# TensorE goes past six stage barriers, and SyncE loads the position bias of a two-layer hybrid backbone

## The chip, the cores and the metric

The kernel runs on one core of one Trainium2 chip. The metric is the device time of one execution in microseconds, as the median of three runs.

## The reference, cut to what matters

Two layers run over 256 context and 256 latent tokens of width 1024, all in float32. Each layer does:

```python
h = rms_norm(x, g1) * (1 + sc1) + sh1             # the same for the context
p = h @ w_in                                       # feeds three mixers and three merge gates
y_a = mlstm_branch(...)                            # chunkwise mLSTM, both directions
y_b = mla_branch(...)                              # latent attention with a rotary part
y_c = natten_branch(...)                           # neighbourhood attention with a position bias
y = (sig(g_a) * y_a + sig(g_b) * y_b + sig(g_c) * y_c) @ w_out
x = x + g1 * y
x = x + g2 * (relu(norm2(x) @ w_ff1) ** 2 @ w_ff2)
```

In the neighbourhood attention a latent query row adds a bias to its scores against the latent keys, and a mask shuts out columns beyond its window:

```python
bias = rpb[:, dr_idx[None, :, None], dc_idx[:, None, :]]
s_win = q @ k_band * scale + bias
s_win = where(col_ok, s_win, NEG_INF)
s_ctx = q @ k_ctx * scale                          # no bias, no mask
p = softmax(concat([s_win, s_ctx]))
```

The last layer computes latent tokens only; its context serves as keys and values.

## The kernel before, in words

Every product is made from float32r halves: a weight block `raw` is split into `wH` (ScalarE, line 710) and `wL = raw - wH` (GpSimd, lines 579 and 581; for some blocks VectorE does the first part, line 1082), and TensorE forms `wH*xH + wH*xL + wL*xH`. Weight blocks pass through a ring of 17 quarters of 256 columns. A 1 MB block (eight quarters) of the neighbourhood attention, `na` 0 to 5, so finds room for two at a time. SyncE loads the blocks in one written order (`load`, line 484); a block's load waits until the block that held its place is split, and its split waits until TensorE has used that block.

A layer is a row of stages, each written out by hand for each engine: `ml` (mLSTM), `na`, `mla`, and then without barriers between them the merge (`to`, `wo`) and the MLP (`ff`). At the end of `ml`, `na` and `mla`, in each of two layers, ScalarE, VectorE, GpSimd and TensorE all call `end()`: a drain that adds 1 to the semaphore `phase_end` and a wait until it holds 4 for each barrier so far (function `barrier`, lines 558 to 561). A seventh one stands at the end of the kernel. SyncE waits on `phase_end` in one place only (in `load_gate`, before it loads gate tiles of the merge into memory that the `mla` stage used).

GpSimd splits blocks ahead before it comes to `end()`: at the end of `ml` it splits `na` 0 and then `na` 1, at the end of `na` the block `dq` 1, while VectorE at the end of `mla` makes the first parts of four `to` blocks. TensorE waits before each product for its weights (`w_split`, `w_share`) and before it fills a bank for the bank's last reader (`bank_free`).

The `na` stage: units 0 to 5 are the products with `na` 0 to 5 (lines 1665 on), queries first, then keys, then values. ScalarE squares each bank (line 956), VectorE sums and scales it (lines 1397, 1413, 1422), and TensorE turns it round (line 1849). Then come the attention steps (scores at line 1888). At the start of the stage ScalarE issues 12 DMAs for the bias table `a_tb` (line 869; 128 KB each, rows of 64 floats), since that memory holds mLSTM values until the barrier. VectorE waits for all 12 and adds the mask in one instruction over 3072 columns (line 1314) before it sums any bank. The table is read at line 1461, in the attention steps of latent tiles.

Of the kernel before, what the change touches and what calls it, by code (L numbers as in the profile page):

```python
# [25 lines left out]
ALU = mybir.AluOpType  # L26
# [258 lines left out]
def build(nc, a, out):  # L285
    ctx = ExitStack()
    with ctx:
# [187 lines left out]
        def _(sp):  # L475
# [19 lines left out]
            def load_gate(l, T):  # L495
# [14 lines left out]
                    sp.wait_ge(*S(f"gate_out{k}").at(16 * KC * (l + 1)))  # L510
                sp.dma_start(dst, g_spill[K, :, lat]).then_inc(S(f"gate_in{c % 2}" if branch == 2 else f"gate_b{c}").handle, 16)

            def load_all(name, l, js):
                for j in js:
                    load(name, l, j)
# [12 lines left out]
            for l in range(DEPTH):  # L528
                if l:
                    load_all("ml", l, range(7))  # L530
                cn = gate_range(l, "cn").start
                for T in range(cn):
                    load("gate", l, T)
                    if l == 0 and T in (3, 4, 7, 8):
                        load_mod(MOD_PROJ + (3, 4, 7, 8).index(T))
                load_all("na", l, range(6))
                load_all("ns", l, range(KC))
                for key in KEYS[N["dq", l, 0]:N["ms", l, 0]]:
                    load(*key)
                load_all("ms", l, range(KC))  # L540
                load_all("to", l, range(4))
                for branch in (2, 1):
                    for c in range(KC):
                        load_gate(l, TURN.index((branch, c)))
                load_all("wo", l, range(4))
                for j in range(32):
                    load("ff", l, j)
                    if l == 0:
                        for m in ff_mods(j - 2):
                            load_mod(m)  # L550
# [93 lines left out]
        def _(act):  # L644
# [147 lines left out]
            for l in range(DEPTH):  # L792
# [63 lines left out]
                for br in ("na", "mla"):  # L856
# [2 lines left out]
                    nb = list(norm_banks(br, l))  # L859
                    if br == "na":  # L860
                        act.preload_act_table_set("sqrt_and_others")
                        for j in range(6):
                            for up in range(2):

                                src = bass.AP(a["na_rpb"].tensor,
                                              a["na_rpb"].offset + l * HEADS * RPB_R * RPB_C
                                              + (WIN_R - GRID_H + 1 + j - up) * RPB_C + WIN_C - GRID_W,
                                              [[1, GRID_W], [RPB_R * RPB_C, HEADS], [1, GRID_W]])
                                act.dma_start(a_tb[64 * up:64 * up + 64, :, j, :], src)\
                                    .then_inc(S(f"na{l}_rpb").handle, 16)  # L870
                    if br == "mla":
                        for j in range(3):
                            ahead(N[("dq", l, j) if j < 2 else ("dk", l, 0)])
# [177 lines left out]
        def _(dve):  # L1051
# [121 lines left out]
            for l in range(DEPTH):  # L1173
# [129 lines left out]
                for br in ("na", "mla"):  # L1303
# [3 lines left out]
                    if br == "na":  # L1307
                        dve.tensor_scalar(gcols[:, 0:1], par[:, l, R_NGQ:R_NGQ + 1], NA_SCALE, None, ALU.mult)
                        dve.tensor_copy(gcols[:, 1:2], par[:, l, R_NGK:R_NGK + 1]).then_inc(S(tag + "g").up(1), 1)
                        kk = S(tag + "g").n  # L1310
                        dve.wait_ge(*S(tag + "rpb").at(12 * 16))
                        mask = const[:, C_MASK:C_MASK + GRID_W].rearrange("p (a w) -> p a w", a=1)
                        tb = a_tb.rearrange("p h j w -> p (h j) w")
                        link(dve.tensor_tensor(tb, tb, mask.broadcast_to([P, 48, GRID_W]), ALU.add))
                    else:
                        dve.memset(gcols[:, 0:1], MLA_SCALE)
                        link(dve.memset(gcols[:, 1:2], 1.0))
                        dve.tensor_scalar(gcols[0:64, 0:1], par[0:64, l, R_GQ:R_GQ + 1], MLA_SCALE, None, ALU.mult)
                        dve.tensor_copy(gcols[0:64, 1:2], par[0:64, l, R_GK:R_GK + 1]).then_inc(S(tag + "g").up(1), 1)
                        kk = S(tag + "g").n  # L1320

                        free(dve.tensor_copy(l_c[:, 4, :], full(u0 + 2, 0)[:, :]), u0 + 2, 0)
                        freed(u0 + 2, 0)
                        free(dve.tensor_tensor(l_c[:, 4, :], l_c[:, 4, :], full(u0 + 2, 1)[:, :], ALU.add), u0 + 2, 1)
                        freed(u0 + 2, 1)
                        dve.wait_ge(*S(tag + "cstd").at(2))
                        for c in range(5):
                            lo = t0 if c < 3 else 0
                            dve.scalar_tensor_tensor(l_c[:, c, lo:], l_c[:, c, lo:],
                                                                      par[:, l, R_GCQ + c:R_GCQ + c + 1],  # L1330
                                                                      st[:, int(c >= 3), lo:], ALU.mult, ALU.mult).then_inc(S(tag + "cn").up(1), 1)
                        dve.wait_ge(*S(tag + "cn").at(5))
                        for c in range(5):
                            lo = t0 if c < 3 else 0
                            dve.wait_ge(*S(tag + "cH").at(c + 1))
                            dve.tensor_tensor(oL[:, C_AT[c], lo:], l_c[:, c, lo:],
                                                               oH[:, C_AT[c], lo:].bitcast(F32), ALU.subtract).then_inc(S(tag + "cL").up(1), 1)
                        dve.wait_ge(*S(tag + "cL").at(5))
                        for t in range(NTILE):
                            dve.wait_ge(*S(tag + "krs").at(t + 1))  # L1340
                            dve.reduce_sum(stat[:, 32 + t:33 + t], l_t[:, 0:ROPE], axis=AX).then_inc(S(tag + "krsum").up(1), 1)
                            kr = l_kr[:, t:t + 1, :]
                            link(dve.tensor_tensor(kr, small[:, t:t + 1, 32:64], ropeg[:, l, 1:2, :], ALU.mult))
                            if t >= 2:
                                rope(kr, kr, l_r, t - 2, 1)
# [91 lines left out]
                    for m in range(len(nb) + 1):  # L1437
# [4 lines left out]
                        if m >= 2:  # L1442
                            keys_out(m - 2)
                    keys_out(len(nb) - 1)

                    items = [(qi, t, h) for qi, t in enumerate(att_tiles(l)) for h in range(HEADS)]
                    for step in range(len(items) + 3):
# [122 lines left out]

        @block.tensor
        def _(pe):
            phase = [0]

            def end():
                phase[0] += 1
                barrier(pe, phase[0])

            def begin(u, b):

# [123 lines left out]
            for l in range(DEPTH):  # L1704
# [91 lines left out]
                    ins.then_inc(S(tag + "nd").up(1), 1)  # L1796
                square_sums(ML_H - 1)
                gates(l, "last")
                end()
                for br in ("na", "mla"):  # L1800
                    tag = f"{br}{l}_"
                    u0 = U0[br, l]
# [116 lines left out]
                                                   flip if br == "na" else ident)  # L1919
                            ins.then_inc(S(tag + "ot").up(1), 1)  # L1920
                    assert next(extra, None) is None and pace * len(items) >= 12 * KC
                    end()

                for j in range(4):
                    features(N["to", l, j], U0["to", l] + j, 4, both(4, t0), oH, oL)
# [19 lines left out]
                            square_sums2(1, 0, 0, 2 * (j - 5))  # L1945
                if l == 0:
                    square_sums2(1, 0, 0, 6)
            end()
            for k in range(4):
                for c in range(4):  # L1950
                    cc = (k % 2) * 4 + c
# [59 lines left out]
```

## Time and profile before

| | |
|---|---|
| median of three runs | 1999.97 us (1999.17 to 2003.4) |
| the profiled execution's own time | 2001.05 us |
| its span | 1998.9 us |
| TensorE matmul busy | 1706.2 us (85%) |
| VectorE / ScalarE / GpSimd busy | 1034.3 / 835.2 / 671.7 us |
| mean granted TensorE clock | 0.937 |

The profile's page gives busy time by engine, the chain that ended last, and the groups of instructions with the idle time before them. A wait at line 560 is a wait at a stage barrier; the engine named is the one that came last.

### The profile page before, as it was taken

How to read it: one execution, taken by the hardware profiler on the slowest of the kernel's cores; microseconds unless marked ns; L12 is line 12 of the kernel's file. 1: busy time of each engine (PE TensorE's matmuls, PEld its weight loads, DVE VectorE, ACT ScalarE, POOL GpSimd, SP SyncE). 2: the span in 40 equal slices, each digit the busy share in tenths (PEclk: the TensorE clock that was granted, in tenths of full speed). 3: DMA queues.
4: the chain of work that ended last, by engine and by line, in shares of the span. 5: the costliest groups of instructions: out<-in, count | busy, mean ns of one | idle time of the engine just before them, and what ended most of it. 6: DMA issues, size and time to landing. Idle time of an engine off the chain costs nothing.

```text
span 1998.9 us, 24815 instructions
## 1 busy us (share of the span) xinstructions
PE 1706.2 (85%) x9538; PEld 1437.7 (72%) x9538; DVE 1034.3 (52%) x1851; ACT 835.2 (42%) x1474; POOL 671.7 (34%) x420
## 2 busy tenths in 40 slices
PE   2578798899887898889999998978788878879998
PEld 1466576886666666658888886867786666678998
DVE  6797843225324444445868874145134245445565
ACT  3214465334354542243223233268434366435443
POOL 1323322440133300144555543523452333023442
PEclk8789899999998999999999999989899888989999
DMA  6364211420012303214344653121321123154553
GB/s 256 136 232 179 96 37 42 117 85 22 22 61 80 131 23 125 91 43 160 121 182 171 250 211 126 59 95 59 116 85 64 55 88 116 43 182 143 176 188 127
DMA packets 66216, 229.58 MB, mean 115 GB/s; under 512 B 18465, under 2 KB 22707, under 8 KB 52531
## 3 DMA queue, kind: packets, MB, share of 16 engines
q1 hardware_dynamic: 46992, 208.42, 29.4%
q10 hardware_dynamic: 19107, 19.58, 3.0%
q8 instruction: 76, 1.25, 0.2%
q14 instruction: 41, 0.34, 0.1%
HBM read 216.45 MB, written 11.53 MB: 114 GB/s over the span
## 4 chain that ended last, share of the span: by engine, by line
PE 67%; DVE 15%; ACT 8%; issue 4%; POOL 2%; DMA 1%; ACTq 1%; POOLq 1%; DVEq 0%; SPq 0%
PE bank L1609 35%; PE bank L1665 8%; PE bank L1621 6%; PE bank L1909 4%; DVE acc L1100 3%; PE bank L1794 3%; DVE mjunk L1097 3%; PE bank L1888 3%; PE bank L1895 2%; PE bank L1647 2%; ACT wH L710 2%; POOL wL L579 1%; DVE arena L1128 1%; POOL hL L597 1%; PE bank L1849 1%
## 5 line engine op out<-in xcount | busy, mean ns | idle before, releaser
L710 ACT ACTIVATE wH<-raw 128x768 fp32r<-128x768 f32 (+7 forms) x396 | 296.7, 806 | 598.0 <-PE bank L1609 399.8
L579 POOL TENSOR_TENSOR wL<-raw,wH 128x1280 fp32r<-128x1280 f32 (+4 forms) x146 | 300.3, 2057 | 698.2 <-ACT wH L710 698.2
L581 POOL TENSOR_TENSOR wL<-raw,wH 128x768 fp32r<-128x768 f32 (+3 forms) x198 | 319.8, 1615 | 397.6 <-ACT wH L710 397.6
L1609 PE MATMUL bank<-hH,wH 128*128 128x512 f32 (+1 forms) x848 | 302.1, 356 | 88.0 <-DVE hL L1137 34.7
L1609 PE MATMUL bank<-hL,wH 128*128 128x512 f32 (+1 forms) x848 | 296.9, 350 | 0.0
L1609 PE MATMUL bank<-hH,wL 128*128 128x512 f32 (+1 forms) x848 | 296.1, 349 | 0.0
L1609 PEld LDWEIGHTS bank<-hH,wH 128*128 128x128 f32 x848 | 167.7, 198 | 116.9 <-issue 57.0
L1609 PE MATMUL bank<-oH,wH 128*128 128x512 f32 (+1 forms) x576 | 196.6, 341 | 9.9 <-DVEq L560 9.9
L1609 PE MATMUL bank<-oL,wH 128*128 128x512 f32 (+1 forms) x576 | 195.3, 339 | 0.0
L1609 PE MATMUL bank<-oH,wL 128*128 128x512 f32 (+1 forms) x576 | 195.1, 339 | 0.0
L1609 PEld LDWEIGHTS bank<-hH,wL 128*128 128x128 f32 x848 | 167.7, 198 | 19.1
L1609 PEld LDWEIGHTS bank<-hL,wH 128*128 128x128 f32 x848 | 168.0, 198 | 18.5 <-issue 0.5
L1100 DVE SCALAR_TENSOR_TENSOR acc<-acc,cb 128x1024 f32<-128x1024 f32 x96 | 176.7, 1852 | 2.7
L1621 PE MATMUL bank<-hH,wH 128*128 128x512 f32 (+1 forms) x384 | 148.3, 386 | 13.8 <-ACT gst L737 7.9
L1665 PE MATMUL bank<-wH,hH 128*128 128x256 f32 x480 | 140.4, 293 | 17.6 <-POOLq L560 14.8
L1665 PE MATMUL bank<-wL,hH 128*128 128x256 f32 x480 | 138.9, 289 | 0.0
L1665 PE MATMUL bank<-wH,hL 128*128 128x256 f32 x480 | 138.8, 289 | 0.0
L1621 PE MATMUL bank<-hL,wH 128*128 128x512 f32 (+1 forms) x384 | 136.8, 356 | 0.0
L1621 PE MATMUL bank<-hH,wL 128*128 128x512 f32 (+1 forms) x384 | 136.7, 356 | 0.0
L1525 DVE SCALAR_TENSOR_TENSOR arena<-bank,modT,arena 128x256 f32<-128x256 f32 x120 | 54.3, 480 | 140.5 <-PE bank L1609 139.4
L1609 PEld LDWEIGHTS bank<-oH,wH 128*128 128x128 f32 x576 | 110.8, 192 | 22.3 <-DVEq L560 10.3
L1609 PEld LDWEIGHTS bank<-oL,wH 128*128 128x128 f32 x576 | 110.9, 193 | 11.8 <-issue 0.5
(212 smaller groups left out, 3242.1 us busy)
## 6 DMA issues: line engine op xcount, KB each, us to landing
raw<-in_p_ff SPq DMA_DIRECT2D x64, 1024.0 KB, 4.8
acc<-in_p_mod SPq DMA_DIRECT2D x48, 1024.0 KB, 5.4
raw<-in_p_ml SPq DMA_DIRECT2D x12, 1024.0 KB, 6.9
raw<-in_p_na SPq DMA_DIRECT2D x12, 1024.0 KB, 4.8
raw<-in_p_mgc SPq DMA_DIRECT2D x16, 512.0 KB, 3.9
raw<-in_p_mga SPq DMA_DIRECT2D x16, 512.0 KB, 3.5
raw<-in_p_mgb SPq DMA_DIRECT2D x16, 512.0 KB, 3.4
raw<-in_p_out SPq DMA_DIRECT2D x8, 1024.0 KB, 7.8
```

The costliest lines, as they stand in the source:

```text
L579: pool.tensor_tensor(l_[:, 0:cut], r_[:, 0:cut], h_[:, 0:cut].bitcast(F32), ALU.subtract)
L581: pool.tensor_tensor(l_[:, cut:k * w], r_[:, cut:k * w], h_[:, cut:k * w].bitcast(F32), ALU.subtract)\
L710: act.activation(flat(wH, n)[:, part], flat(raw, n)[:, part], ACT.Copy)\
L1097: link(dve.scalar_tensor_tensor(mjunk[:, :], row, 1.0, cb[:, LAT, :], ALU.mult, ALU.mult, accum_out=modT[:, l, chunk, LAT:LAT + 1]))
L1100: ins = dve.scalar_tensor_tensor(row, row, 1.0, cb[:, last, :], ALU.mult, ALU.mult, accum_out=modT[:, l, chunk, last:last + 1])
L1525: ins = dve.scalar_tensor_tensor(x[:, c + b, lo:lo + 256], src[:, lo:lo + 256], modT[:, l, gate + c + b, s:s + 1], x[:, c + b, lo:lo + 256 ...
L1609: ins = pe.matmul(dst, w_[:, kk, c:c + P], r_[:, kk, lo:TOK], start=kk == k0 and m == 0, stop=kk == k0 + kn - 1 and m == 2)
L1621: ins = pe.matmul(bank[gate_bank(l, T)][:, t0:TOK], w_[:, kk, :], r_[:, kk, t0:TOK], start=kk == 0 and m == 0, stop=kk == KC - 1 and m == 2)
L1665: ins = pe.matmul(bk[:, o:o + width], s_[:, at[kk], t * P:t * P + P], w_[:, kk, c:c + width], start=kk == 0 and m == 0, stop=kk == k - 1 a ...
L1794: ins = pe.matmul(bank[bk][:, lo:hi], lhs, m_E[d][:, e_at, 0:hi - lo], start=q == 0, stop=q == len(group) - 1)
L1888: pe.matmul(bank[4 + step % 2][:, 0:nk], q_, k_, start=True, stop=True).then_inc(S(tag + "s").up(1), 1)
L1909: ins = pe.matmul(bank[k % 2][:, 0:P], s_pt[:, k % 2, c * P:c * P + P], v_[:, c, (h // 2) * P:(h // 2) * P + P], start=c == 0, stop=c == n ...
```

## The change

TensorE no longer waits on `phase_end` at the six stage ends. It still adds its 1, so that the other three engines wait for it as before, and then waits for semaphores of the stage it leaves: at the end of `ml` for ScalarE's and VectorE's last work on its banks and for the gates of the `ml` loop; at the end of `na` and `mla` for the last bank of the branch product and for `oL`, which reads the last turned bank. Only at the end of the kernel does it wait on `phase_end` as before. The four other engines' barriers stay.

The 12 bias DMAs move from ScalarE to SyncE, between the loads of `na` 2 and `na` 3, behind a wait until the barrier after `ml` has passed. The mask is added behind the last normalised keys, just ahead of the attention steps.

```diff
+            def load_bias(l):
+
+                for j in range(6):
+                    for up in range(2):
+                        src = bass.AP(a["na_rpb"].tensor,
+                                      a["na_rpb"].offset + l * HEADS * RPB_R * RPB_C
+                                      + (WIN_R - GRID_H + 1 + j - up) * RPB_C + WIN_C - GRID_W,
+                                      [[1, GRID_W], [RPB_R * RPB_C, HEADS], [1, GRID_W]])
+                        sp.dma_start(a_tb[64 * up:64 * up + 64, :, j, :], src).then_inc(S(f"na{l}_rpb").handle, 16)
+
...
-                load_all("na", l, range(6))
+                load_all("na", l, range(3))
+                sp.wait_ge(S("phase_end").handle, 4 * (3 * l + 1))
+                load_bias(l)
+                load_all("na", l, range(3, 6))
...
-                        for j in range(6):
-                            for up in range(2):
...
-                                act.dma_start(a_tb[64 * up:64 * up + 64, :, j, :], src)\
-                                    .then_inc(S(f"na{l}_rpb").handle, 16)
...
-                        dve.wait_ge(*S(tag + "rpb").at(12 * 16))
-                        mask = const[:, C_MASK:C_MASK + GRID_W].rearrange("p (a w) -> p a w", a=1)
-                        tb = a_tb.rearrange("p h j w -> p (h j) w")
-                        link(dve.tensor_tensor(tb, tb, mask.broadcast_to([P, 48, GRID_W]), ALU.add))
...
                     keys_out(len(nb) - 1)
+                    if br == "na":
+                        dve.wait_ge(*S(tag + "rpb").at(12 * 16))
+                        mask = const[:, C_MASK:C_MASK + GRID_W].rearrange("p (a w) -> p a w", a=1)
+                        tb = a_tb.rearrange("p h j w -> p (h j) w")
+                        link(dve.tensor_tensor(tb, tb, mask.broadcast_to([P, 48, GRID_W]), ALU.add))
...
-            phase = [0]
-
-            def end():
-                phase[0] += 1
-                barrier(pe, phase[0])
+            def leave():
+
+                pe.drain().then_inc(S("phase_end").handle, 1)
...
-                end()
+                leave()
+                pe.wait_ge(*S(tag + "std").at(ML_H))
+                pe.wait_ge(*S(tag + "acc").at(2 * ML_H))
+                pe.wait_ge(*S("gate_free").at(GATES * l + gate_range(l, "loop").stop))
...
-                    end()
+                    leave()
+                    pe.wait_ge(*S("branch_free").at(tiles_so_far(br, l) + KC))
+                    pe.wait_ge(*S(tag + "oL").at(len(att_tiles(l))))
...
-            end()
+            leave()
+            pe.wait_ge(S("phase_end").handle, 4 * (3 * DEPTH + 1))
```

## Rows read from the trace of the kernel before

**Rows 1.** The chain that ended last: shares of the span by engine.
```profile
PE 67%; DVE 15%; ACT 8%; issue 4%; POOL 2%; DMA 1%; ACTq 1%; POOLq 1%; DVEq 0%; SPq 0%
```

**Rows 2.** TensorE's waits, whole run: total us, times, longest us.
```profile
PE bank L1665 <- POOLq L560: 14.8, 2, 8.2
PE bank L1609 <- DVEq L560: 9.9, 2, 4.9
PE bank L1609 <- POOLq L560: 7.0, 2, 3.5
PE bank L1849 <- DVE arena L1422: 5.5, 2, 5.0
```

**Rows 3.** Timeline at the first barrier: start us, us, instruction, [idle before].
```profile
350.78 1.82 POOL L581 TENSOR_TENSOR wL<-raw,wH 128x768 fp32r<-128x768 f32 x1
...
356.15 1.80 POOL L581 TENSOR_TENSOR wL<-raw,wH 128x768 fp32r<-128x768 f32 x1
358.06 9.51 ACTq L869 DMA_DIRECT2D arena<-in_na_rpb  x12
358.07 0.58 PE L1665 MATMUL bank<-wH,hH 128*128 128x256 f32 x1 [6.63 <-POOLq L560]
370.48 3.36 DVE L1314 TENSOR_TENSOR arena<-arena,const 128x3072 f32<-128x3072 f32 x1 [12.21 <-DMA arena<-in_na_rpb]
```

**Rows 4.** The chain in order of time, layer 0: start us, us, work.
```profile
358.07 25.47 PE bank L1665 x192
384.41 11.51 PE bank L1665 x96
...
534.14 28.91 PE bank L1609 x120
...
886.01 321.95 PE bank L1609 x1419
```

**Rows 5.** The chain in order of time, layer 1.
```profile
1293.07 1.28 ACT wH L710
...
1299.22 6.01 PE bank L1609 x48
...
1469.62 11.52 PE bank L1665 x96
...
1569.53 22.10 PE bank L1609 x120
```

**Rows 6.** Timeline at the fourth barrier, layer 1, after `ml`.
```profile
1429.16 1.80 POOL L581 TENSOR_TENSOR wL<-raw,wH 128x768 fp32r<-128x768 f32 x1
...
1435.66 10.02 ACTq L869 DMA_DIRECT2D arena<-in_na_rpb  x12
...
1448.98 4.59 DVE L1314 TENSOR_TENSOR arena<-arena,const 128x3072 f32<-128x3072 f32 x1 [13.12 <-DMA arena<-in_na_rpb]
1450.31 4.93 POOL L581 TENSOR_TENSOR wL<-raw,wH 128x768 fp32r<-128x768 f32 x1
```

**Rows 7.** Time to landing: `na` weight blocks in 350 to 400 us, bias DMAs.
```profile
DMA to landing us min/median/max: 4.7/5.1/5.9
...
DMA to landing us min/median/max: 3.4/3.9/5.9
```

**Rows 8.** Timeline of VectorE at the first attention scores of layer 0.
```profile
437.77 0.43 DVE L1465 TENSOR_REDUCE stat<-bank 128x1 f32<-128x256 f32 x1 [14.96 <-PE bank L1888]
```

**Rows 9.** Timeline of VectorE ahead of the second barrier, after `na`.
```profile
531.38 0.69 DVE L1482 TENSOR_TENSOR oL<-bank,oH 128x512 fp32r<-128x512 f32 x1 [1.38 <-ACT oH L1004]
```

**Rows 10.** Timeline at the third and sixth barriers, after `mla`.
```profile
781.20 3.55 DVE L1082 TENSOR_TENSOR wL<-raw,wH 128x768 fp32r<-128x768 f32 x4
...
802.39 1.62 DVE L1502 TENSOR_TENSOR acc<-acc,arena 128x512 f32<-128x512 f32 x1
...
810.05 0.69 DVE L1502 TENSOR_TENSOR acc<-acc,arena 128x512 f32<-128x512 f32 x1
...
1758.46 2.00 ACT L710 ACTIVATE wH<-raw 128x1280 fp32r<-128x1280 f32 x2 [18.22 <-DMA raw<-in_p_out]
```

More of the change, by code:

```diff
@@ L861, in _ @@
                         act.preload_act_table_set("sqrt_and_others")
-                        for j in range(6):
-                            for up in range(2):
[L865 to L868, printed above, removed]
-                                act.dma_start(a_tb[64 * up:64 * up + 64, :, j, :], src)\
-                                    .then_inc(S(f"na{l}_rpb").handle, 16)
                     if br == "mla":
```

## The prediction

> **What bounds the kernel now.** I read the page's chain first: TensorE holds 67% of it [rows 1], and a matmul is running for 85% of the span. So time can only be saved where TensorE stands still or runs at its lower clock. Second, the list of its waits [rows 2]. The six stage barriers cost it 14.8 + 9.9 + 7.0 = 31.7 us, two waits for each kind of stage end. In four of them GpSimd came last, in two VectorE. A fourth entry, 5.0 us before a turn (line 1849), is one wait of layer 1. These 37 us are the ground that the change can work on. Third, the timelines at each barrier, to see what TensorE could have started on, since a wait that goes is replaced by the next one.
>
> **Barrier 1, after `ml` of layer 0.** TensorE waits 6.63 us until GpSimd has split `na` 0 and then `na` 1 [rows 3]. Unit 0 needs only `na` 0, done at 350.78 + 1.82 = 352.60. The three new waits are for work of ScalarE and VectorE that was over before. So unit 0 starts at about 352.7 and not at 358.07: 5.4 us. `na` 1 is done at 357.95 and unit 1 wants it only 11.5 us after 352.7. The first two units take 25.47 us for 192 matmuls, later ones 11.51 for 96 [rows 4], so 25.47 - 23.02 = 2.4 us went to the lower clock (1.2 GHz of 2.4) after the 6.6 us of idling. With only 1.2 us of idling left I expect the clock to stay up. Sum 7.8 us; bounds 5.4 (clock still falls) and 7.9.
>
> Who could spoil this? Behind the start stand ScalarE, whose squares no longer queue behind 9.51 us of DMA issue, and VectorE, which no longer waits for the bias: both only get earlier. `na` 2 is loaded before the new wait on SyncE. `na` 3 is not: it now stands behind the barrier (358.0) and 12 DMA issues. SyncE has no such DMA in this trace; the nearest row is ScalarE's own issue, 9.51 and 10.02 us for 12, and I take that. `na` 3 is then issued at 367.6 and lands 5.1 us later [rows 7], at 373. TensorE uses `na` 1 up to 352.7 + 23.0 = 375.7, and only then may `na` 3 be split, so its load is covered by 3 us; and from raw data to TensorE a split takes 1299.22 - 1293.07 = 6.15 us [rows 5], half of what unit 2 covers. Cost in layer 0: nothing; without the cover it would be each microsecond of lateness beyond 381.
>
> **Barrier 4 and the start of `na` in layer 1.** `na` 0 is split at 1429.16 + 1.80 = 1430.96 [rows 6]; TensorE starts at 1435.67 after 8.2 us [rows 2] of waiting. Here units 0 and 1 have half the rows (48 matmuls each), so the stage is tight. Before, the bias came in at 1448.98, the mask took VectorE 4.59 us, GpSimd's split beside it took 4.93 in place of 1.80, and TensorE waited 5.0 us for VectorE [rows 2, 6]. All that goes: ScalarE and VectorE are free from 1435.6. Unit 3 started at about 1469.4 [rows 5]. Now units 0 to 2, 192 matmuls, need 23.0 us at full clock, plus 0.7 for the turns, plus at most the 2.4 that layer 0 lost: from 1431.0 that is 1454.7 to 1457.1. The other condition is `na` 3: issued at 1435.6 + 9.6 = 1445.2, landed at 1450.3, split 6.1 later, at 1456.5 to 1457. The DMA decides here. Gain at unit 3: 1469.4 - 1457 = 12.4; because nothing covers a late load here I take 11.5. Bounds: 12.5, and 8.6 if the load lands 3 us later. The nearest thing to that is a queue that gives `na` 3 nothing until the bias has landed: last issue at 1444.6, landed 3.9 later [rows 7] at 1448.5, then 5.1 to 5.9 for the block: 1454.4 at worst, 4 us later than my value.
>
> The Trainium skill, page "DMA: Bandwidth & Descriptors", section "Queues, rings and completion order", speaks against this step: an engine's hardware queue is one ring on each transfer engine, taken in ring order, while different queues are served in turn. By it the weight block that shared the engines with the bias before (ScalarE's queue and SyncE's) stands behind it now. By that rule layer 1 gains 3 us less and layer 0 nothing less; by a plain 5.1 us after issue it is the sum above.
>
> **The mask in its new place.** VectorE idles 14.96 us before the first scores [rows 8]; 3.4 to 4.6 us of mask fit in that, also with GpSimd slowed by 3 us beside it, since its next small blocks are used in the attention steps only. Cost 0; without cover 4.6 a layer. In layer 1 the gap is of the same kind.
>
> **Barriers 2 and 5, after `na`.** `oL` ends at 531.38 + 0.69 = 532.07 [rows 9], TensorE started at 534.14, and its weights `dq` 0 were split long before. It now starts at 532.15: 2.0 us. At barrier 5 the same rows stand 1035.3 us later: 2.1. The clock: 120 matmuls took 28.91 us, at the rate of the MLP (321.95 / 1419 = 0.227) they take 27.2, so 1.7 was lost [rows 4]; in layer 1 72 of 256 columns at 0.12 and 48 at 0.227 make 19.5, against 22.10 [rows 5], 2.6 lost. Idling falls from 3.4 to 1.4 us, in a stretch where TensorE was thinly used just before. I take half back, 0.9 and 1.3, with bounds of 0 and all. Sum 2.9 + 3.4 = 6.3; bounds 4.1 and 8.4.
>
> **Barriers 3 and 6, after `mla`.** TensorE waits 4.9 us each for VectorE, whose four `to` splits take 3.55 us from 781.20 [rows 10]. It needs only the first (0.9): start at 782.1, not 784.86, 2.75 us. In layer 0 VectorE is next late: tied up until 802.39 + 1.62 = 804.0 by a split whose block lands no earlier, it then needs three more pairs of 1.4 us and ends at 808.3 and not 810.74. 2.4 us. In layer 1 nothing: the merge waits for the block of `w_out`, which lands at 1758.46 after 18.2 us of ScalarE's waiting [rows 10] and is issued behind SyncE's own `phase_end`, which VectorE still sets. Bounds 1 and 2.75 for the pair.
>
> **The sum.** 7.8 + 11.5 + 6.3 + 2.4 = 28.0 us. The profiled execution's own time was 2001.05 (span 1998.9 and 2.15 around it), so it would be 1973.0; it stood 1.1 above the median, so I name 1972. Everything between the barriers is paced by TensorE, so an earlier start is carried on; the MLP of 322 us without a break [rows 4] shows it best. All lower bounds together, 5.4 + 8.6 + 4.1 + 1.0 = 19.1, give 1981; all upper ones, 7.9 + 12.5 + 8.4 + 2.75 = 31.5, 1968.
>
> **Rivals.**
> - *The clock is given nothing and `na` 3 is late.* The starts move but the clock falls as before, and the load waits for the bias to land. For it: `na` 3 is the one transfer moved behind 1.5 MB of short rows. Against: idling at barrier 1 falls to a fifth. 5.4 + 8.6 + 4.1 + 2.4 = 20.5: 1979.5.
> - *Given back.* TensorE comes early to banks and blocks that others release no earlier, as in layer 1's merge, and only the mask's 5.0 us is kept: 1995. For it: barrier 6. Against: in `na` the next releases (squares, splits) hang on TensorE's own banks.
> - *SyncE's bias issue blocks the weights (the other side).* Place: `na` 3 behind 12 DMAs. If SyncE needs much longer than ScalarE's 9.5 us for them, TensorE waits for unit 3. Unit 3 started at about 396.5 in layer 0 (384.41 + 11.51 and the turns [rows 4]) and 1469.4 in layer 1; the load must be issued by 385 and 1458, so from about 25 us of issue the two `na` stages lose, and, with the 8.7 us of the other barriers against it, from about 29 the kernel does. At 38 us (four times ScalarE's): unit 3 at 407 and 1485, 10.5 + 15.5 - 8.7 = 17 slower: 2017. For it: SyncE's rate for such short rows isn't in the trace. Against: ScalarE's queue took 9.5 and 10.0 for the same transfers.
> - *TensorE does not get past.* A wait that I take as long over is not: a new wait stands behind GpSimd as `phase_end` did. Again only the mask: 1995.
>
> **Chances.** Forecast 70% (its own spread 1968 to 1977); clock and load 18%; given back 6%; blocked weights 3%; not past 3%. The 80% range is 1967.5 to 1983. About 0.2% (4 us) is what a measurement can tell from no change: faster 94%, same 3%, slower 3%.
>
> **What would show each step.** Right: line 560 gone from TensorE's waits; unit 0 starting within 0.2 us of the end of the first `na` split; 192 matmuls in about 23.0 us in layer 0; no wait of line 1849 in layer 1's first turn; unit 3 of layer 1 starting on GpSimd's split, with ScalarE's line 710 waiting for the DMA of `na` before it; barrier 6's gain eaten by `w_out`. Wrong: a wait of line 1888 for the mask; `na` 3 issued more than 12 us after the barrier; the first units after barriers 2 and 5 as slow as before; an early start followed by an equal wait at the next turn.

## The result and the profile after

The changed kernel takes 1979.5 us (median of 4 runs, 1977.6 to 1981.4) against 2001.7 us of the kernel before (4 runs, 1999.2 to 2003.6): ratio 0.989, 95% interval 0.987 to 0.991. The forecast of 1972 is 7.5 us too low. The 80% range (1967.5 to 1983) holds the time, the forecast's own spread (1968 to 1977) doesn't. The profiled execution's own time is 1979.92 us, its span 1977.8, so the span fell by 21.1 us where the steps promised 28.0.

TensorE's waits in the changed kernel, to be read against [rows 2] (engine, line and what it waited for: total us, times, longest):

```profile
PE bank L1612 <- DVE hL L1520: 18.1, 2, 10.5
...
PE bank L1668 <- POOL wL L594: 10.5, 5, 3.7
...
PE bank L1612 <- DVE wL L1086: 5.0, 2, 2.5
...
PE bank L1612 <- DVE oL L1487: 2.9, 2, 1.5
```

The three entries for a barrier, six waits in all, and the one for layer 1's turn are gone. In their place stand the data waits of the stages' first units: GpSimd's split (line 594), VectorE's split (1086), the last `oL` (1487). The largest of those shown is `hL` (1520), which ends the merge; it stood there before too (17.8 us in two waits, the longest 11.5). Ends of the `mla` stages, both layers, timeline of TensorE:

```profile
775.34 0.47 PE L1612 MATMUL bank<-oH,wH 128*128 128x512 f32 x1 [2.48 <-DVE wL L1086]
...
806.61 0.77 PE L1612 MATMUL bank<-hH,wH 128*128 128x512 f32 x1 [7.63 <-DVE hL L1520]
...
1721.31 0.55 PE L1612 MATMUL bank<-oH,wH 128*128 128x256 f32 x1 [2.48 <-DVE wL L1086]
...
1748.58 0.55 PE L1612 MATMUL bank<-hH,wH 128*128 128x256 f32 x1 [10.51 <-DVE hL L1520]
```

TensorE leaves after the first of VectorE's four splits, as forecast, 2.48 us after its last work and not 4.9. Then it waits 7.63 and 10.51 us at the end of the merge (6.31 and 11.54 before).

The first barrier, timelines of GpSimd, TensorE, SyncE (its DMA issues), ScalarE and VectorE, answering to [rows 3] and [rows 8]:

```profile
353.47 1.82 POOL L594 TENSOR_TENSOR wL<-raw,wH 128x768 fp32r<-128x768 f32 x1
...
355.54 0.36 PE L1668 MATMUL bank<-wH,hH 128*128 128x256 f32 x1 [1.41 <-POOL wL L594]
...
360.86 8.16 SPq L521 DMA_DIRECT2D arena<-in_na_rpb  x12
369.06 4.80 SPq L484 DMA_DIRECT2D raw<-in_p_na  x2
...
362.15 0.60 ACT L960 ACTIVATE arena<-bank 128x512 f32<-128x512 f32 x1
...
418.00 3.35 DVE L1449 TENSOR_TENSOR arena<-arena,const 128x3072 f32<-128x3072 f32 x1
418.04 4.18 POOL L592 TENSOR_TENSOR wL<-raw,wH 128x384 fp32r<-128x384 f32 x1
...
433.61 0.42 DVE L1470 TENSOR_REDUCE stat<-bank 128x1 f32<-128x256 f32 x1 [12.26 <-PE bank L1894]
```

TensorE starts 0.25 us after the first split. The mask fits ahead of the first scores with 12.26 us to spare, though the GpSimd split beside it takes 4.18 us (its neighbours of the same size take 1.01).

The chain in order of time, whose pieces answer to [rows 4] and [rows 5] (start us, us, work, number of instructions):

```profile
355.54 23.27 PE bank L1668 x192
378.81 0.87 PE bank L1855 x8
379.69 11.51 PE bank L1668 x96
...
528.30 27.46 PE bank L1612 x120
...
1424.86 8.70 PE bank L1668 x48
...
1439.82 11.78 PE bank L1668 x96
1451.60 0.44 PE bank L1855 x4
1452.04 11.52 PE bank L1668 x96
...
1549.86 21.27 PE bank L1612 x120
```

192 matmuls in 23.27 us: the clock stayed up (25.47 before). After the `na` stages the 120 matmuls take 27.46 and 21.27 us, not 28.91 and 22.10. Layer 1's `na` start, answering to [rows 6]: SyncE's issues, ScalarE's split of `na` 3 and GpSimd's end of it:

```profile
1429.36 8.74 SPq L521 DMA_DIRECT2D arena<-in_na_rpb  x12
1438.14 11.84 SPq L484 DMA_DIRECT2D raw<-in_p_na  x3
1443.51 2.01 ACT L723 ACTIVATE wH<-raw 128x1280 fp32r<-128x1280 f32 x2 [2.99 <-DMA raw<-in_p_na]
...
1447.77 1.86 POOL L594 TENSOR_TENSOR wL<-raw,wH 128x768 fp32r<-128x768 f32 x1
```

The weight blocks that SyncE issued between 1436 and 1440 us, from the view of their tile:

```profile
DMA to landing us min/median/max: 5.3/5.8/6.3
```

`na` 3 is issued behind the twelve bias DMAs and split 5.4 us later; it is ready at 1449.6, and TensorE wants it at 1452.04. It never waits for it.

**Where the missing microseconds went.** By the marks in both traces the steps brought 27.8 us (table further down). The rest was lost between them. The largest piece stands in a stage that the change doesn't touch, the `ml` stage of layer 1 from its first matmul to the last head's. Its row in the view by stretches, first the kernel before, then the changed one (stretch: length, busy time of each engine, granted clock, DMA share, GB/s):

```profile
1246.10:1415.80 169.70, 141.80 (x896) 128.62 (x896) 64.67 (x143) 98.51 (x165) 68.09 (x59) 0.91 0.22 75
```

```profile
1236.50:1410.30 173.80, 146.66 (x896) 132.89 (x896) 64.51 (x143) 98.52 (x165) 68.00 (x59) 0.89 0.21 73
```

The same 896 matmuls are busy 4.9 us longer, the other four engines the same to 0.2 us. The trace's record of the granted clock, which has two levels, 1.2 and 2.4 GHz, puts 29.7 us of this stage at 1.2 GHz before and 37.5 after. That was the open question for the experiments: is this the change's doing, or that of the moment at which the stage begins?

### The profile page after: what moved, and what is told of

It is laid out like the page before. It is cut to its first block, busy times and chain, and to the rows that moved or that the text cites. A ratio compares the mean times of both kernels' runs of the same rounds, so it can differ in the third digit from the quotient of the medians.

```text
span 1977.8 us, 24823 instructions
## 1 busy us (share of the span) xinstructions
PE 1707.5 (86%) x9538; PEld 1437.1 (73%) x9538; DVE 1032.7 (52%) x1851; ACT 835.3 (42%) x1474; POOL 674.6 (34%) x420
## 4 chain that ended last, share of the span: by engine, by line
PE 67%; DVE 15%; ACT 9%; issue 4%; POOL 2%; DMA 2%; ACTq 1%; DVEq 0%; SPq 0%
PE bank L1612 34%; PE bank L1668 8%; PE bank L1624 6%; PE bank L1915 4%; DVE acc L1104 3%; PE bank L1797 3%; DVE mjunk L1101 3%; PE bank L1894 3%; PE bank L1901 2%; PE bank L1650 2%; ACT wH L723 2%; DMA raw<-in_p_out 1%; DVE arena L1132 1%; POOL hL L610 1%; PE bank L1855 1%
## 5 line engine op out<-in xcount | busy, mean ns | idle before, releaser
L592 POOL TENSOR_TENSOR wL<-raw,wH 128x1280 fp32r<-128x1280 f32 (+4 forms) x146 | 306.8, 2101 | 674.3 <-ACT wH L723 674.3
```

Source lines behind the costliest of these rows:

```text
L592: pool.tensor_tensor(l_[:, 0:cut], r_[:, 0:cut], h_[:, 0:cut].bitcast(F32), ALU.subtract)
```

## The experiments

Every kernel ran beside the kernel before on its chip, and its ratio is to those runs (their medians were 2001.1 to 2004.5 us, so ratios compare better than medians). "ml 1" is the length of the stage just shown and, in brackets, how much of it was at 1.2 GHz. The last column says how long before the stage's first matmul the granted clock fell to 1.2 GHz, by the same record.

| kernel | median us | ratio (95%) | ml 1 us | clock fell ahead of it, us |
|---|---|---|---|---|
| before, first and second trace | 2002.1 (second) | 1.000 (0.999 to 1.001) | 169.6 (29.7), 169.6 (29.7) | 5.9, 5.8 |
| changed, first trace | 1979.5 | 0.989 (0.987 to 0.991) | 173.8 (37.5) | 3.4 |
| after_again | 1980.4 | 0.990 (0.988 to 0.992) | 173.9 (37.6) | 3.3 |
| bar_only | 1991.8 | 0.996 (0.994 to 0.997) | 169.9 (30.0) | 5.3 |
| bias_only | 1996.9 | 0.997 (0.996 to 0.998) | 169.6 (29.7) | 5.9 |
| bias_last | 1981.0 | 0.990 (0.988 to 0.991) | 173.9 (37.6) | 3.4 |
| pad2 | 1976.5 | 0.986 (0.985 to 0.988) | 170.0 (30.0) | 5.2 |
| pad5 | 1985.0 | 0.991 (0.989 to 0.992) | 173.3 (36.8) | 4.2 |
| wo_early | 1969.7 | 0.983 (0.982 to 0.985) | 169.6 (29.6) | 6.0 |
| wo_again (the same kernel) | 1969.9 | 0.984 (0.983 to 0.986) | 171.1 (31.5) | 6.1 |
| wo_mid | 1975.5 | 0.987 (0.986 to 0.988) | 171.2 (31.5) | 6.1 |
| before_pad1 | 2005.7 | 1.001 (1.000 to 1.003) | 172.2 (35.7) | 3.3 |
| wo_before | 2001.3 | 0.999 (0.998 to 1.000) | 169.6 (29.7) | 5.9 |

**The changed kernel again (after_again).** No edit.

> The changed kernel once more, whole. The six steps at the barriers measured 27.8 us in the first pair of traces (7.4, 3.4, 2.6, 11.2, 2.8, 0.4), but the time fell by 22.2: outside the steps the changed kernel's trace is 2.7 us later at the end of the first mLSTM stage, 0.9 in the first neighbourhood attention, 1.1 and 2.3 at the start and in the second mLSTM stage. Theory A (the lower TensorE clock falls in other places from run to run, nothing of the change): the six steps repeat within 1 us each, the four losses outside do not repeat in the same places, ratio 0.986 to 0.990. Theory B (the change itself costs these 7 us, by where its shifts put TensorE's idle spells): the same four losses of about the same size stand in this trace too, ratio 0.989.

The same ratio, and the same 173.9 us with 37.6 at the lower clock. Up to TensorE's arrival at the first barrier the first trace took 354.1 us, this one 350.9, the two traces of the kernel before 351.4 and 352.7. So the start-up was scatter and the `ml` 1 loss is not. The spans are equal all the same (1977.8 and 1977.6 us): of the 3.2 us that the second trace gains there it loses 1.7 in layer 1's `mla` stage, which has 39.4 us at 1.2 GHz and not 34.3, and 0.8 behind the last merge. What a stage takes in a single trace is thus good to 2 or 3 us, unless it repeats as `ml` 1's does.

**The barriers alone (bar_only).** The position bias back on ScalarE's queue and the mask ahead of the keys, in the changed kernel:

```
+                        for j in range(6):
+                            for up in range(2):
+                                ...
+                                act.dma_start(a_tb[64 * up:64 * up + 64, :, j, :], src)
```

> Barriers alone: TensorE passes the six barriers, ScalarE issues the bias DMAs and the mask is added first, as before. Theory A (the steps as predicted): layer 0 keeps all but about 1 us of its 7.4 at the first barrier, because the mask ends at about 374 on the clock of the trace before and TensorE's first turn wants VectorE by 376. Layer 1 keeps nothing at the fourth barrier: TensorE starts 4.7 us earlier and then waits about 10 for the mask, unit 3 starts where it did. Sum 6.4 + 3.4 + 2.6 + 0 + 2.8 = 15 less whatever is lost outside: ratio 0.9925 to 0.995. Rival (parts add up, the mask's own wait of 5.0 us is all that the bias is worth): 22 - 5 = 17 faster, ratio 0.9915, and TensorE's wait before the turn stays 5 us.

It gained 8.6 us (0.4%, interval 0.3 to 0.6), less than the 0.5% to 0.75% that I had expected. Layer 1 in its timelines of ScalarE's queue, VectorE, GpSimd and TensorE shows why:

```profile
1426.81 10.97 ACTq L879 DMA_DIRECT2D arena<-in_na_rpb  x12
1437.88 0.38 ACT L966 ACTIVATE arena<-bank 128x256 f32<-128x256 f32 x1 [9.80 <-issue]
...
1440.40 5.19 DVE L1324 TENSOR_TENSOR arena<-arena,const 128x3072 f32<-128x3072 f32 x1 [13.39 <-DMA arena<-in_na_rpb]
...
1442.34 4.92 POOL L591 TENSOR_TENSOR wL<-raw,wH 128x768 fp32r<-128x768 f32 x1
...
1447.11 0.69 PE L1860 MATMUL bank<-const,arena 128*128 128x128 f32 x2 [11.58 <-DVE arena L1432]
```

TensorE crosses the barrier early and then waits 11.58 us for VectorE at the first turn, because the bias is issued, landed and masked as late as ever. In layer 0 the same costs 3.11 + 0.77 us. Counted from TensorE's arrival at the barrier, unit 3 starts 1.7 us earlier than in the kernel before in layer 0, where I had expected 6.4, and 2.1 us later in layer 1, where I had expected no change; that is the miss. An earlier start without the bias's move is a wait moved by one unit: my "given back" rival, true for this half of the change.

**The bias alone (bias_only).** The kernel before with the bias loaded by SyncE (behind `phase_end`, ahead of `na` 3) and the mask behind the last keys; the barriers stay.

> Bias and mask alone: all engines keep the six barriers, SyncE loads the bias and the mask is added last. Theory A: layer 0 gains nothing (TensorE never waited for the mask there); layer 1 loses the wait of 5.0 us before the turn and the 1.2 us of lower clock behind it, unit 3 starts about 6.6 us earlier: ratio 0.9967. With the barriers alone at 15 that leaves some 5 us that need both parts. Rival (only the wait itself): 5 us, 0.9975. Rival (weights behind the bias in SyncE's queue cost something): a wait of TensorE or ScalarE for the load of the fourth block appears in layer 1, 0.999 or more.

5.8 us by the ratio, as expected. Layer 1's turn no longer waits, and units 0 to 2 take 26.9 us, not 33.7. The parts together, 8.6 + 5.8 = 14.4, fall 6 us or more short of the whole change's 20 to 22, though the whole has the `ml` 1 loss of 4.2 us and neither part has it. Each of the three is known to some 3 us. So part of the gain comes only where both are there, and the 11.58 us above are the largest place of it.

**The bias behind the weights (bias_last).** The rule that would make `na` 3 late behind the bias can be tried by putting all six `na` blocks first:

```
-                load_all("na", l, range(3))
+                load_all("na", l, range(6))
                 sp.wait_ge(S("phase_end").handle, 4 * (3 * l + 1))
                 load_bias(l)
-                load_all("na", l, range(3, 6))
```

> The changed kernel with the bias DMAs behind the load of the last of the six blocks (na 5) in place of ahead of the fourth: no weight block stands behind the barrier or the bias. Theory A: the fourth block (na 3) lands early, ScalarE's wait of 3.0 us for it in layer 1 goes, but TensorE did not wait for it (its split was done at 1449.6, unit 3 started at 1451.8), so the time stays within 0.5 us of the changed kernel. Rival (the load decides unit 3, as the prediction held): 2 to 3 us faster. Rival (the bias now lands late, since na 5 is issued about 32 us after the barrier and the mask must be on before the first scores 60 us after it): it still lands 20 us before, no cost.

No gain: 0.990 both. The place of `na` 3 behind the bias costs nothing.

**Work added ahead of the stage (pad2, pad5).** Two or five matmuls on TensorE near the end of layer 0's MLP; their result is overwritten by the next sum:

```
                         if l == 0 and i == 3 and j > 4:
+                            if j == 5:
+                                pe.wait_ge(*S("nrm10_sq").at(1))
+                                for _ in range(2):
+                                    pe.matmul(bank[4][:, 0:TOK], ones, n_sq[:, 0, 0:TOK], start=True, stop=True)
                             square_sums2(1, 0, 0, 2 * (j - 5))
```

> The changed kernel with two matmuls of 512 columns added on TensorE (their result is overwritten) near the end of the layer-0 feed-forward stage, where TensorE is never waiting: 2 x 0.43 = 0.86 us, all of it before the layer-1 mLSTM stage. In the three traces with the whole change that stage (start and heads) has 37.6 us at the lower granted clock, in the kernel before 29.7, and it is 4.2 us longer there (95.08 + 78.78 against 93.96 + 75.67). Theory B: the work of the stage is the same, and how much of it gets the lower clock hangs on when the stage begins; a later start by 0.86 us then changes the 37.6 us at the lower clock, by anything up to the 8 us between the traces (some 4 us of time), and the kernel ends between 3.5 us faster and 2 us slower than the changed kernel. Rival: the change itself leaves TensorE idle longer in that stage, whatever its start; then 37.6 us stay, and the kernel is 0.9 us slower than the changed one (ratio to before 0.9898 + 0.0004).

> The same with five matmuls, 5 x 0.43 = 2.15 us before the layer-1 mLSTM stage. Theory B: the start lies then where it lay in the kernel with the barriers alone, which had 30.0 us at the lower clock in this stage; I expect 28 to 32 us here, the stage 3.5 to 4.5 us shorter than in the changed kernel, and the total 1.3 to 2.3 us below the changed kernel's (ratio to before 0.988 to 0.9892). Rival (the stage's own waits set the lower clock, not its start): 37.6 us stay, and the total is 2.2 us above the changed kernel's (ratio 0.991).

One such matmul is two matmul records in the trace and costs 0.84 us, twice what I had reckoned: the MLP stage grew from 368.13 to 369.81 and 372.39 us. With 1.7 us of work more, the kernel is faster than the changed one (0.9864, interval 0.9848 to 0.9879, against 0.9898, 0.9880 to 0.9917), and the stage is back to 170.0 us. Between pad2's span and that of the changed kernel's first trace, 1971.9 and 1977.8 us, the stage accounts for 3.8 us less the pad's 1.7. The start-up, which scatters, is 5.1 us shorter (349.0 against 354.1 us up to the first barrier), and 1.4 us are lost again in other stages.

```profile
1232.90:1402.90 170.00, 142.32 (x895) 129.00 (x895) 64.56 (x143) 98.41 (x165) 68.19 (x59) 0.91 0.22 75
```

With 4.3 us more it has 36.8 us at the lower clock again, and the kernel is 1.4 us slower than the changed one by the ratios, 5.1 by the spans. The stage's work is the same in all; only what stands ahead of it changed. My guess for pad5, 28 to 32 us at the lower clock and a gain, was made with half the length of the five and missed. Together the two show that the loss comes and goes with what is put ahead of the stage. That the change itself makes TensorE idle more in this stage is refuted by pad2.

**The same on the kernel before (before_pad1).** One such matmul, 0.84 us.

> The kernel before, untouched but for one matmul of ones on the squares (f32, two passes, 0.84 us by the length that two and five of them gave the layer-0 feed-forward stage: 1.68 and 4.26 us) near the end of that stage. Theory B (what part of the layer-1 mLSTM stage gets the lower granted clock hangs on when the stage begins, in the kernel before as in the changed one): this puts the stage where it lies in the changed kernel, so its start and heads get about 37.6 us at the lower clock in place of 29.7 and take 173.9 us in place of 169.6; the kernel is 0.84 + 4.2 = 5 us slower than the one before (4 to 6; ratio 1.002 to 1.003). Rival (the extra lower clock is the changed kernel's own, from its missing barriers or moved loads): 29.7 us stay and the kernel is 0.84 us slower (ratio 1.0004).

The stage: 172.2 us with 35.7 at the lower clock, from 169.6 with 29.7, though this kernel has all its barriers:

```profile
1250.80:1423.00 172.20, 145.09 (x896) 131.78 (x896) 64.61 (x143) 98.54 (x165) 68.15 (x59) 0.90 0.22 74
```

That is 2.6 of the 4.2 us expected. The total, +2.8 us with an interval of +0.6 to +5.2, fits 0.84 + 2.6 but doesn't exclude the rival's 0.84; the stage's own row does.

What decides is not the time from the start of the span. The stage begins at 1236.5 us in the changed kernel's first trace (its row stands above) and at 1236.8 in bar_only, yet they differ by 4 us; and so do after_again and wo_early, which begin at 1233.7 and 1233.6. The rows of bar_only, after_again and wo_early:

```profile
1236.80:1406.70 169.90, 142.24 (x895) 128.92 (x895) 64.59 (x143) 98.41 (x165) 68.14 (x59) 0.91 0.22 75
...
1233.70:1407.60 173.90, 146.77 (x896) 133.02 (x896) 64.59 (x143) 98.53 (x165) 68.09 (x59) 0.89 0.21 73
...
1233.60:1403.20 169.60, 141.76 (x896) 128.61 (x896) 64.56 (x143) 98.50 (x165) 68.00 (x59) 0.91 0.22 75
```

Nor does TensorE do anything else at the entrance: in all fourteen traces it idles from 8.2 to 4.2 us ahead of the stage's first matmul. What differs is when, beside this same work, the granted clock falls (last column of the table). Where it fell 5.2 to 6.1 us ahead, 29.6 to 31.5 us of the stage are at 1.2 GHz; where it fell 3.3 to 4.2 us ahead, 35.7 to 37.6. Between the first traces of the kernel before and of the changed one, 2.4 of the 7.8 us lie in this first spell, which reaches further into the stage, and 5.4 in later ones. A pad moves the fall against the work: 1.7 us moved it from 3.4 to 5.2, and 0.84 us in the kernel before from 5.9 to 3.3. What sets the moment of the fall no run shows.

**The load of w_out (wo_early, wo_again).** The merge's last arrival, taken out of its place behind the guarded gate loads:

```
                 for branch in (2, 1):
                     for c in range(KC):
+                        if (branch, c) == (1, 2):
+                            load_all("wo", l, range(1))
                         load_gate(l, TURN.index((branch, c)))
-                load_all("wo", l, range(4))
+                load_all("wo", l, range(1, 4))
```

> The changed kernel, where SyncE issues the load of the first w_out block ahead of the six gate loads that wait for the third and sixth barrier, not behind them. In the changed kernel that load is issued 6.4 us after the barrier's crossing by TensorE (774.5 to 780.9) and lands at 792.3, ScalarE waits 18.81 us for it, VectorE is idle 4.03 us before it can split it (789.6 to 793.7) and TensorE waits 7.63 us for VectorE's hL in layer 0; in layer 1 17.82, 3.86 and 10.51 us. Theory A (w_out is the last to arrive in both merges, so that the sixth barrier's removal was worth 0.4 us rather than 2 or 3): both idle times go, 4.0 + 3.9 us, less up to 1 us that the gates' own landing still costs in layer 1 (the 6.15 us wait for it stands); the kernel is 6 to 8 us faster than the changed one, ratio to before 0.9858 to 0.9868. Rival: VectorE's own merge sets the end (its operations from 785.5 on and the modulation after them), and w_out's landing only fills a hole that GpSimd's contention would take anyway: under 2 us, ratio 0.989 to 0.990.

> The fastest kernel so far again (the changed kernel with the first w_out block ahead of the guarded gate loads). Theory B: what it gained over the changed kernel is 4.2 us in the layer-1 merge, some 0.5 us in the layer-0 merge, and 4.3 us because its layer-1 mLSTM stage has 29.6 us at the lower clock rather than 37.6. The first is bound to repeat (to-matmuls to w_out 23.0 us, not 27.2), the last does if the stage's start repeats: 0.983 (0.9815 to 0.985), and 0.986 if not. Rival: its lead over the changed kernel was mostly the chance of one chip: 0.986 to 0.990.

The best version: 1969.7 and 1969.9 us, by the ratios 10 to 13 below the changed kernel, more than the 6 to 8 that I had expected, and only half of it for my reason. The merge of layer 1 from its first matmul to w_out's first went from 27.2 to 23.0 and 23.4 us; its timeline in wo_early (SyncE, ScalarE, VectorE, TensorE):

```profile
1714.97 0.33 SPq L484 DMA_DIRECT2D raw<-in_p_out  x1
1716.70 2.84 SPq L511 DMA_DIRECT2D arena<-g_spill  x6
...
1722.50 2.01 ACT L725 ACTIVATE wH<-raw 128x1280 fp32r<-128x1280 f32 x2 [10.06 <-PE bank L1614]
...
1725.39 0.42 DVE L1506 SCALAR_TENSOR_TENSOR arena<-arena,bank 128x256 f32<-128x256 f32 x1 [4.84 <-DMA arena<-g_spill]
...
1737.27 0.55 PE L1614 MATMUL bank<-hH,wH 128*128 128x256 f32 x1 [8.05 <-DVE hL L1522]
```

ScalarE no longer waits for w_out's landing but for TensorE to free the space. In layer 0 the whole merge, to the MLP's first matmul, gained only 0.4 to 0.6 us (92.36 against 92.81 and 93.00 in the two traces of the changed kernel): there the rival was right, VectorE's own work and a gate that lands 3.66 us late take w_out's place. Another 4.3 us came from the `ml` 1 stage, back at 169.6 us; in the second trace of the same kernel it has 171.1, so this part isn't secure.

**w_out in the middle (wo_mid)**, behind the first two guarded gates.

> The changed kernel with the first w_out block issued behind the first two of the six guarded gate loads. With w_out ahead of all six, VectorE waits 3.66 us (layer 0) and 4.84 us (layer 1) for a gate to land, while ScalarE could split w_out only at 785.9 in layer 0 anyway (TensorE frees the space then). Theory: the two gates land before w_out, these waits shrink to 1 to 2 us, w_out lands some 2 us later, which layer 0 hides and layer 1 does not quite; net 1 to 3 us faster than with w_out first, unless the layer-1 mLSTM stage falls back to the extra lower clock (then 1 to 3 us slower); ratio 0.982 to 0.983. Rival: what VectorE gains at the gates it loses waiting for w_out's split, same time within 1 us as with w_out first (0.983 to 0.9835).

A miss: 0.987, not 0.982 to 0.983. VectorE's wait for the gate falls to 1.41 us, but it then waits 2.54 for a later gate and 2.96 for ScalarE's split of w_out. Layer 1's merge takes 25.3 us, so w_out first is the better order; 1.6 us of the distance to wo_early are the `ml` 1 stage's.

**The same in the kernel before (wo_before, before_again).**

> The kernel before, with the load of the first w_out block ahead of the six guarded gate loads. In the changed kernel the same move brought the layer-1 merge 4.2 us (27.22 to 22.99 from the first to-matmul to the first w_out matmul) and the layer-0 merge 0.5 us net, and moved the layer-1 mLSTM stage off the extra 7.9 us of lower clock. Theory: here too some 5 us, all from the merges (4.2 in layer 1, 0.5 to 1 in layer 0), nothing from the mLSTM stage, which has no extra lower clock in the kernel before: ratio 0.9975 (0.997 to 0.998). The whole change, put on top of it (the kernel with the early w_out load, ratio 0.9832), is then worth 28 to 29.5 us, the sum of the predicted steps. Rival: the barrier's own wait covers w_out's landing in the kernel before, so the move is worth under 2 us here (ratio 0.999 to 1), and the gain of the early load belongs to the changed kernel alone.

> The kernel before, unchanged, for a second trace of it. In the two kernels that equal it up to the layer-1 mLSTM stage or the layer-0 merge, the query down-projection of MLA in layer 0 took 58.4 and 58.3 us with 19.9 us of it at the lower granted clock; in its own trace 53.15 us with 2.97. If the kernel before falls to either from one execution to the next, this trace shows 53 or 58 us there, and its own median stands anywhere in 1998 to 2007 us; then the early w_out load brought the kernel before its 3.6 us in the layer-1 merge in that trace, and the total hid it. If it shows 53 us and so do its times (ratio 1.000), the longer stage belongs to the two edited kernels, which no theory of mine explains. Its layer-1 mLSTM start and heads: 169.6 us with 29.7 at the lower clock, as before, by theory B.

The total says 1.6 us, interval -4.2 to +0.8, and cannot tell 5 from nothing. The traces can, in part: the layer-1 merge fell from 25.2 to 21.6 us, and a stage ahead of the edit, the query down-projection of layer 0, rose from 53.2 to 58.3:

```profile
534.50:592.80 58.30, 52.10 (x179) 37.15 (x179) 10.66 (x36) 21.27 (x35) 10.09 (x8) 0.83 0.15 47
```

This kernel and before_pad1 are the kernel before up to there, and both show 58.3 us at a granted clock of 0.83; the two traces of the kernel before show 53.1 and 0.97. Every engine but TensorE is busy equally long. I know no way in which the edits could act so early. The record of the granted clock points at the same thing as in `ml` 1. In the edited pair the clock fell 0.60 and 0.61 us ahead of this stage's first matmul, and 19.9 us of the stage are at 1.2 GHz; in the two traces of the kernel before and in bias_only it fell 0.44, 0.53 and 0.57 us ahead, and 2.8 to 3.0 us are. The nearest two of these falls are 0.03 us apart, no run moved the fall here, and the edited pair also shares a chip, so this is argued and not shown. Whether the early w_out pays with barriers standing stays open.

## Why the prediction was right, and where it was short

Each step, predicted and measured between the same marks of the two traces:

| step | predicted us | measured us |
|---|---|---|
| barrier 1, start and clock | 7.8 | 7.4 |
| barrier 4, bias and mask in layer 1 | 11.5 | 11.2 |
| barriers 2 and 5 | 2.9 + 3.4 | 3.4 + 2.8 |
| barrier 3 | 2.4 | 2.6 |
| barrier 6 | 0 | 0.4 |
| sum | 28.0 | 27.8 |

- *Barrier 1.* The start and the clock both as said. 192 matmuls took 23.27 us; the 2.2 us of it that were the clock's came back since TensorE idled 1.41 and not 6.63 us. All the traces bear this out: the five with 6.63 us of idling have 5.0 to 6.1 us at 1.2 GHz in units 0 to 2, the nine with 1.4 us none, but for bar_only (3.4), which waits again at the first turn.
- *Barrier 4.* Right in size, wrong in what decides. SyncE's issue took 8.7 us where I had used 9.6 from ScalarE's rows, and ScalarE did wait for the DMA of `na`. But "The DMA decides here" failed: unit 3 started on TensorE's own pace and not on GpSimd's split, 2.4 us after it was ready. Units 0 to 2 took 27.2 us, over the 23.7 + 2.4 that I had allowed at most, 2.9 of it because the 48 matmuls of unit 0 took 8.70 us and not the 5.8 of full clock. That the sum still came within 0.3 us is in part luck: I had taken off 0.9 us for a late load that didn't come. From the ring order in the Trainium skill's page "DMA: Bandwidth & Descriptors" (section "Queues, rings and completion order") I had drawn a rival by which the block behind the bias lands 3 us later. It landed 5.3 us after its issue, where blocks with nothing ahead of them took 4.7 to 5.9 [rows 7], and bias_last gained nothing. This refutes my 3 us and not the ring order: the last bias DMA was issued 0.6 us ahead of the block, and the bias DMAs landed within 2.9 to 4.3 us of their issue.
- *Barriers 2 and 5.* Half of the lost clock back was a choice between ends; it was right in sum, 6.2 for 6.3.
- *Barriers 3 and 6.* What was given back at barrier 6 stood in the forecast: w_out's block. wo_early shows it by taking the block away from the end of the line.
- *The step that failed* is the sentence under the sum, "Everything between the barriers is paced by TensorE, so an earlier start is carried on". It is true of the work and not of the clock. The stage of 896 matmuls in layer 1 took 4.2 us more for the same work: it does so in both traces of the changed kernel and in bias_last, in neither half alone, and not with 1.7 us of work put ahead of it. The other 2.5 us between 27.8 and the 21.1 measured in the span are small pieces: 2.7 us more up to the first barrier and 0.8 in layer 0's `na` stage, less 0.9 behind `ml` 1. In the second trace of the same kernel the first of these is a gain of 0.5 us, and as much is lost in other places.
- *The base.* I took 1.1 us off since the profiled execution stood that much above the median of three runs. With more runs the kernel before has medians of 2001.1 to 2004.5 on five sets of runs, so nothing should have been taken off. 1.0 + 6.9 (28.0 less 21.1 in span), less 0.4 for the median after, is the miss of 7.5.

The result fell on the number of my first rival, 1979.5, and that rival was wrong in both its halves: the clock came back at barrier 1 and `na` 3 was not late. Only the traces tell the two apart. In the chances, the rivals "given back" and "TensorE does not get past" both stand at 1995, 5 us faster, yet the one is counted under faster and the other under the same.

## What to carry to other kernels

Before counting on a wait that goes, ask of the next thing what its own last arrival is: the barriers alone gave 8.6 us, since the bias was as late as ever, and the last one nothing, since a weight block was queued behind its guard; both parts with that block moved to the front gave 32 to 34. Add up a change of 1% by stages in both traces, not only by its own steps, since a stage that nobody touched can move by 4 us with what stands ahead of it. When such a stage shows the same work at another clock, look where the clock falls against its first matmul, and put a microsecond or two of matmuls whose result nobody reads ahead of it, before believing in any cause inside it.

## What the runs showed of the hardware

- The layer-1 `ml` stage, with the same instructions, had between 29.6 and 37.6 us at 1.2 GHz in fourteen traces, the larger amounts (35.7 and more) all where the clock fell 3.3 to 4.2 us ahead of its first matmul and the smaller ones (31.5 and less) all where it fell 5.2 to 6.1 us ahead. Adding 1.7 us of matmuls brought it from 37.5 to 30.0.
- SyncE issues the 12 bias DMAs in 8.2 and 8.7 us, ScalarE in 9.5 to 11.0; behind the six weight blocks SyncE's took 9.2 and 10.2.
- While VectorE adds the mask, a GpSimd split takes 4.18 us in place of 1.01 (changed kernel, layer 0) or 4.92 in place of 1.8 (bar_only, layer 1); the mask takes 3.35 us in the first case and 5.19 in the second. In both the split grows by 3.1 to 3.2 us, close to the mask's own 3.35; in the second the mask began 2.0 us before an earlier split of GpSimd ended and grew by 1.8.
- An f32 matmul of 512 columns on ones and squares is two matmul records that start 0.43 us apart: two such in pad2 made the stage 1.68 us longer, 0.84 each.
